# Scores of both heads in two adjacent PSUM banks, and one Exp over both, in a hybrid gMLP and attention decoder block

## The chip, the cores and the metric

The kernel runs on one Trainium2 chip, as one program on 8 cores. Each core has half of the sequence of one of the four batch entries (2048 positions) and takes the other half, or zeros, as the keys and values that lie before its own. The time is the device time in microseconds (us) of the slowest core.

## What is computed

One layer of a decoder block, cut to what matters here:

```python
h = _rmsnorm(x, norm_g[l])
proj = jnp.einsum('bsd,dn->bsn', h, w_in[l])
...
ya = _gmlp_sgu(a_u, a_v, a_ws[l], a_bs[l], a_ln_g[l], a_ln_b[l]) * jax.nn.silu(a_gate)
...
for p, (window, dilation) in enumerate(B_PATTERNS):      # (128, 1), (512, 4), (2048, 16)
    q = _rmsnorm(qkv[:, :, p, 0], qn_g[p])
    k = _rmsnorm(qkv[:, :, p, 1], kn_g[p])
    o, lse = _dilated_window(q, k, qkv[:, :, p, 2], window, dilation)
...
merged = jax.nn.sigmoid(g_a) * ya + jax.nn.sigmoid(g_b) * yb
x = x + jnp.einsum('bsd,de->bse', merged, w_out[l])
```

The attention is causal, over a window of 128 keys back at dilation 1, 4 or 16, with 8 heads of 64 columns; the outputs of the three patterns are mixed by their softmax denominators.

## The kernel before

The program is written out in order by Python, without a scheduler: each call of `c.op` (L95) puts one instruction on one engine and, where it depends on another engine, a wait on that engine's counter. PE, ACT and DVE run their own lists strictly in that order.

**Stages.** First the rows of x are normalised and transposed (`p0_task`, L343: ACT L354 to L358, DVE L360, eight PE transposes L370, DVE copy L372). Then come 12 attention steps, one for each of four pairs of heads (`hp`) and each of three patterns (`p`); they fill the profile to about 620 us. Behind them stand the gMLP branch (`a1_...`, `a2_task`), the merge (`c1_task`) and the output projection (`fin_task`).

**A step** (`step_tasks`, L432) is made of three kinds of task:

- a *q/k task* (`qk_task`, L386), 9 or 12 in a step: 8 matmuls of 512 columns into one bank (L300), ACT squares it (L393). Later its second part: one PE matmul L400 sums the squares into a second bank, ACT takes Ln (L402, from that bank) and Exp (L404), and DVE scales the first bank into `qT` or `kT` (L407). Only then are both banks given back.
- a *V task* (`v_s1`, L469), 5 or 8 in a step: 32 matmuls of 128 columns into one bank (L300), and DVE casts it into `Vaug` (L485).
- an *attention task* (`att`, L492), 8 in a step, 96 in all: 8 score matmuls L506 for a pair of blocks, those of head h into bank `sb[h]`; ACT takes Exp of each bank (L510, two activations of 128x512); DVE multiplies by the mask (L520, two). Later its second part: 8 matmuls L533 into one bank, which DVE copies or adds to `acc` (L543, L545).

**What sets the order.** `Pipe.submit` (L193) runs a task's first part and then the second parts that have become due; a q/k task's is due two tasks later, an attention task's three to five. The main loop (L687) lets the V and attention tasks of a step alternate with the q/k tasks of the next; every third task it slips in the end of a head pair (`fin_tasks`, ACT L587 to L589, DVE L590 to L594). Twelve of these ends lie inside attention steps.

**Banks.** PSUM has eight banks, in a `FreeList` (L175, L265): `get` takes the one that has been free longest, `put` adds one at the end.

```python
    def get(self):
        assert self.free, "pool exhausted (pipeline too deep for the buffer count)"
        return self.free.pop(0)
    def put(self, it):
        self.free.append(it)
```

`put` is called while the program is written, as soon as the bank's last reader has been recorded, so a bank can be handed out again long before that reader has run. The next PE group that writes it then waits on the chip for the reader (`_deps`, L86, takes in every reader of the buffer).

Of the kernel before, what the change touches and what calls it, by code (L numbers as in the profile page):

```python
# [5 lines left out]
F32 = mybir.dt.float32  # L6
BF16 = mybir.dt.bfloat16
ALU = mybir.AluOpType
AF = mybir.ActivationFunctionType


class Buf:
    __slots__ = ("name", "w", "r", "dsem", "dcnt")

    def __init__(self, name):
        self.name = name
        self.w = None
        self.r = []
        self.dsem = None
        self.dcnt = 0  # L20
# [154 lines left out]
class FreeList:  # L175
# [3 lines left out]
# [5 lines that stand above are left out]
        self.free.append(it)  # L184


class Pipe:

    def __init__(self):
# [43 lines left out]
def build_program(needed=None):  # L233
    nc = bass.Bass("TRN2", target_bir_lowering=False)
# [14 lines left out]
    c = Ctx(nc, needed)  # L249
    ar = Arena(nc)  # L250
    pipe = Pipe()
    PE, ACT, DVE, POOL, SP = c.pe, c.act, c.dve, c.pool, c.sp
    tn, sc, ve, gp = nc.tensor, nc.scalar, nc.vector, nc.gpsimd
# [8 lines left out]
            items.append((t_, b_))  # L262
        return FreeList(items), off

    banks = FreeList([(nc.alloc_psum_tensor(f"pb{i}", [128, 512], F32), Buf(f"pb{i}")) for i in range(8)])  # L265

    off = 0
    cb_t, b_cb, off = ar.alloc("cbf", [128, C_W], BF16, off)
# [163 lines left out]
    def step_tasks(hp, p, prefetch=True, buf=0, att_lag=3):  # L432
# [6 lines left out]
        if True:  # L439
# [51 lines left out]
            for q0 in range(0, len(qblocks), 2):  # L491
                def att(q0=q0):  # L492
                    pair = qblocks[q0:q0 + 2]
                    S = {}

                    def s1():
                        E, b_E0 = S["E"] = E_pool.get()
                        b_Eb = [b_E0, E_extra[id(b_E0)]]
                        sb = [banks.get(), banks.get()]
                        for bi, (r, cc) in enumerate(pair):  # L500
                            for pc in range(2):
                                for h in range(2):
                                    rows = slice(64 * h, 64 * h + 64)
                                    k0 = 128 * (cc + pc)
                                    o_ = (bi * 2 + pc) * 128
                                    c.op(PE, lambda: tn.matmul(sb[h][0][:, o_:o_ + 128], kv[rows, r, k0:k0 + 128],  # L506
                                                               qv[rows, r, 128 * cc:128 * cc + 128], start=True, stop=True),
                                         reads=[b_kT, b_qT], writes=[sb[h][1]], inc=(bi == len(pair) - 1 and pc == 1))
                        for h in range(2):
                            c.op(ACT, lambda: sc.activation(E[:, h].rearrange("p b c q -> p (b c q)"), sb[h][0][:],  # L510
                                                            AF.Exp, scale=8.0),
                                 reads=[sb[h][1]], writes=b_Eb)
                        for bi, (r, cc) in enumerate(pair):
                            mk = maskH if cc == 0 else maskN
                            ev = E[:, :, bi].rearrange("p h c q -> p h (c q)")
                            if False:
                                c.op(POOL, lambda: gp.tensor_tensor(ev, ev, mk.rearrange("p (h x) -> p h x", h=2), ALU.mult),
                                     reads=[b_Eb[bi], b_cb], writes=[b_Eb[bi]])
                            else:
                                c.op(DVE, lambda: ve.tensor_tensor(ev, ev, mk.rearrange("p (h x) -> p h x", h=2), ALU.mult),  # L520
                                     reads=[b_Eb[bi], b_cb], writes=[b_Eb[bi]])
                        banks.put(sb[0]); banks.put(sb[1])

                    def s2():
                        E, b_E0 = S["E"]
                        b_Eb = [b_E0, E_extra[id(b_E0)]]
                        po, b_po = banks.get()
                        for bi, (r, cc) in enumerate(pair):
                            for h in range(2):
                                for pc in range(2):  # L530
                                    blk = r * (nbo + 1) + cc + pc
                                    o_ = (bi * 2 + h) * 128
                                    c.op(PE, lambda: tn.matmul(po[:, o_:o_ + 128], Vaug[:, blk, h, :], E[:, h, bi, pc, :],  # L533
                                                               start=(pc == 0), stop=(pc == 1)),
                                         reads=[b_Vg[blk // 4], b_Eb[bi]], writes=[b_po],
                                         inc=(pc == 1 and h == 1 and bi == len(pair) - 1))
                        (r0, c0), (r1, c1) = pair
                        t00 = r0 + 128 * d * c0
                        t01 = r1 + 128 * d * c1
                        av = bass.AP(acc, t00, [pacc, [t01 - t00, 2], [T, 2], [d, 128]])  # L540
                        ov = po[:].rearrange("p (b h q) -> p b h q", b=2, h=2)
                        if p == 0:
                            c.op(DVE, lambda: ve.tensor_copy(av, ov), reads=[b_po], writes=[b_acc])  # L543
                        else:
                            c.op(DVE, lambda: ve.tensor_tensor(av, ov, av, ALU.add), reads=[b_po, b_acc], writes=[b_acc])  # L545
                        E_pool.put(S["E"]); banks.put((po, b_po))

                    need = max(r * (nbo + 1) + cc + 1 for (r, cc) in pair) // 4
                    return need, (lambda: pipe.submit(s1, s2, lag=att_lag, tag="att"))
                atasks.append(att())  # L550
            nv = 0
# [135 lines left out]
    for n in range(2, 12):  # L687
        hp, p = steps[n]
# [365 lines left out]
```

How the kernel before makes its waits and increments, by code:

```python
    def _wait(self, eng, toks):  # L64
        best = {}
        for t in toks:
            if t is None:
                continue
            sem, val, src = t
            if src is self.pe and eng is self.pe:
                continue
            k = id(sem)
            if eng.seen.get(k, 0) >= val:
                continue
            if k not in best or best[k][1] < val:
                best[k] = (sem, val, src)
        for k, (sem, val, src) in best.items():
            if src is None:
                actual = val
            else:
                self.waited.setdefault(src.name, set()).add(val)
                actual = val if self.rank is None else self.rank[src.name][val]
            eng.h.wait_ge(sem, actual)
            eng.seen[k] = val
# [10 lines left out]
    def op(self, eng, fn, reads=(), writes=(), inc=True):  # L95
        self._wait(eng, self._deps(reads, writes))
        ins = fn()
        if inc:
            eng.cnt += 1
            if self.needed is None or eng.cnt in self.needed.get(eng.name, ()):
                ins.then_inc(eng.sem, 1)
            tok = (eng.sem, eng.cnt, eng)
        else:
            tok = (eng.sem, eng.cnt + 1, eng)
        for b in reads:
            b.r.append(tok)
        for b in writes:
            b.w = tok
            b.r = []
        return tok
```

## Time and profile before

| | us |
|---|---|
| median of 3 runs (1087.00 to 1088.76) | 1087.82 |
| the profiled execution's own time | 1086.05 |
| its span on the slowest core, core 4 | 1085.0 |
| spans of the eight cores | 1074.1 to 1085.0 |
| PE busy | 959.8 |
| DVE busy | 607.5 |
| ACT busy | 536.6 |
| mean granted TensorE clock of the cores | 0.954 to 0.962 |

The span runs from the first to the last instruction of the program. A granted clock of 1 stands for 2.4 GHz, one of 0.5 for 1.2 GHz; between the two it is a mean over both. Busy time of PE is that of matmuls that overlap each other in the pipe, so eight matmuls of 512 columns stand as one row of 1.89 us at the full clock.

### The profile page before, as it was taken

The page shows a single profiled execution, that of the slowest core. Times are in us where ns is not written, and L with a number is a line of the kernel's source. Part 1 is how long each engine was busy: PE and PEld are TensorE (multiplying, and loading weights), DVE is VectorE, ACT ScalarE, POOL GpSimd, SP SyncE. Part 2 cuts the span into 40 slices and gives each one's busy share as a digit, 9 for nine tenths or more (in the row PEclk, how much of TensorE's full clock was granted, in tenths as well). Part 3 has the DMA queues.
Part 4 walks back from the last instruction along what each step waited for, and adds up shares of the span by engine and source line. Part 5 has one row for each costly group of instructions (what it writes and reads, how often), then busy time and mean ns, then how long its engine had stood idle before and what let it go on. Part 6 is the DMA issues. An engine that isn't in the chain of part 4 may idle for free.

```text
span 1085.0 us, 20753 instructions; the slowest of 8 cores (1074.1 to 1085.0 us)
## 1 busy us (share of the span) xinstructions
PE 959.8 (88%) x7264; PEld 543.4 (50%) x7264; DVE 607.5 (56%) x894; ACT 536.6 (49%) x946; POOL 161.9 (15%) x161
## 2 busy tenths in 40 slices
PE   2668769997899979999798978789999999999898
PEld 1336454664556646666466734444444344444343
DVE  6636794557675677756776766656553222222243
ACT  5656867657676686766866464443332111111100
POOL 2000000010000100000010000015454333331100
PEclk9779889999899998999999989889999999999999
DMA  9943521040330403303066000004453933441198
GB/s 237 212 100 60 117 69 18 4 41 1 31 31 2 40 2 30 31 2 30 1 89 79 1 1 1 1 1 40 40 54 52 94 34 35 46 47 11 59 293 270
DMA packets 101622, 62.57 MB, mean 58 GB/s; under 512 B 88720, under 2 KB 92816, under 8 KB 101520
## 3 DMA queue, kind: packets, MB, share of 16 engines
q0 software_dynamic: 91728, 26.61, 24.9%
q1 hardware_dynamic: 7344, 25.71, 7.1%
q10 hardware_dynamic: 2448, 8.91, 2.8%
q8 instruction: 61, 1.00, 0.4%
q14 instruction: 41, 0.34, 0.1%
HBM read 79.44 MB, written 8.39 MB: 81 GB/s over the span
## 4 chain that ended last, share of the span: by engine, by line
PE 67%; ACT 11%; DVE 9%; DMA 6%; issue 6%; DVEq 0%; POOL 0%; ACTq 0%; POOLq 0%; SPq 0%
PE pb L300 59%; DMA wr<-w_in 4%; PE pb L533 3%; ACT lr L402 3%; PE pb L506 2%; ACT lr L404 2%; DVE sta L745 2%; DVE hb L360 1%; PE pb L400 1%; DMA xt<-xh 1%; ACT junk L354 1%; PE pb L370 1%; ACT vg L743 1%; DMA wout<-w_out 1%; DVE kT L407 1%
## 5 line engine op out<-in xcount | busy, mean ns | idle before, releaser
L300 PE MATMUL pb<-hTo,wr 128*128 128x512 bf16 x1920 | 448.5, 386 | 14.6 <-DVE hTo L372 7.6
L300 PEld LDWEIGHTS pb<-hTo,wr 128*128 128x128 bf16 x1920 | 185.6, 99 | 231.0 <-issue 29.5
L119 POOL DMA_DIRECT2D wr<-w_in x72 | 63.8, 894 | 494.2 <-PE pb L300 226.3
L510 ACT ACTIVATE E<-pb 128x512 bf16<-128x512 f32 x192 | 113.0, 592 | 44.5 <-PE pb L506 34.5
L393 ACT ACTIVATE sq<-pb 128x512 bf16<-128x512 f32 (+1 forms) x120 | 69.7, 583 | 109.6 <-PE pb L300 108.1
L300 PE MATMUL pb<-wr,hTo 128*128 128x128 bf16 x1536 | 114.7, 230 | 2.1 <-DVE acc L543 1.9
L300 PEld LDWEIGHTS pb<-wr,hTo 128*128 128x128 bf16 x1536 | 104.0, 123 | 8.2 <-issue 5.1
L934 DVE SCALAR_TENSOR_TENSOR m<-ta,pb 128x512 f32<-128x512 f32 x32 | 22.0, 688 | 148.0 <-PE pb L300 148.0
L407 DVE SCALAR_TENSOR_TENSOR kT<-pb,cf,lr 128x512 bf16<-128x512 f32 (+1 forms) x72 | 70.6, 981 | 57.0 <-ACT lr L404 47.2
L520 DVE TENSOR_TENSOR E<-E,cbf 128x512 bf16<-128x512 bf16 x192 | 72.7, 420 | 30.2 <-ACT E L510 29.2
L402 ACT ACTIVATE lr<-pb,cf 128x512 f32<-128x512 f32 (+1 forms) x120 | 81.1, 676 | 5.4 <-PE pb L400 3.9
L404 ACT ACTIVATE lr<-lr 128x512 f32<-128x512 f32 (+1 forms) x120 | 74.6, 622 | 11.3 <-ACT lr L402 0.4
L927 ACT ACTIVATE ta<-pb 128x512 f32<-128x512 f32 x32 | 19.1, 597 | 120.6 <-PE pb L300 120.6
L407 DVE SCALAR_TENSOR_TENSOR qT<-pb,cf,lr 128x512 bf16<-128x512 f32 x48 | 47.4, 988 | 55.3 <-ACT lr L404 52.3
L545 DVE TENSOR_TENSOR acc<-pb,acc 128x512 f32<-128x512 f32 x64 | 72.3, 1130 | 1.4 <-PE pb L533 1.2
L837 POOL TENSOR_TENSOR gu<-gu,sa 128x512 f32<-128x512 f32 x32 | 40.7, 1271 | 186.5 <-ACT gu L824 130.4
L300 PE MATMUL pb<-wr,hTh 128*128 128x128 bf16 x672 | 57.9, 232 | 6.1 <-DVE acc L543 5.7
L533 PE MATMUL pb<-E,Vaug 128*128 128x128 bf16 x768 | 60.5, 224 | 2.5 <-DVE qT L407 1.6
L370 PE MATMUL pb<-cbf,hb 128*128 128x128 bf16 x256 | 25.6, 263 | 41.8 <-DVE hb L360 39.9
L506 PE MATMUL pb<-qT,kT 64*128 64x128 bf16 x768 | 42.4, 222 | 21.4 <-DVE kT L407 17.1
L300 PE MATMUL pb<-yaT,wr 128*128 128x512 bf16 x256 | 60.5, 379 | 0.0
L300 PE MATMUL pb<-Wv,hTo 128*128 128x512 bf16 x256 | 59.9, 392 | 0.0
(77 smaller groups left out, 1072.3 us busy)
## 6 DMA issues: line engine op xcount, KB each, us to landing
wr<-w_in POOLq DMA_DIRECT2D x72, 256.0 KB, 6.0
xt<-xh SPq DMA_DIRECT2D x16, 512.0 KB, 3.9
xf<-xo ACTq DMA_DIRECT2D x16, 512.0 KB, 5.4
out<-ot SPq DMA_DIRECT2D x16, 512.0 KB, 5.1
xt<-xo SPq DMA_DIRECT2D x12, 512.0 KB, 9.8
xtx<-xo SPq DMA_DIRECT2D x4, 512.0 KB, 12.3
Wv<-w_in POOLq DMA_DIRECT2D x2, 1024.0 KB, 10.9
wr<-w_oa POOLq DMA_DIRECT2D x8, 256.0 KB, 6.4
```

The costliest lines, as they stand in the source:

```text
L119: eng.h.dma_start(out=out, in_=in_, **kw).then_inc(owner.dsem, 16)
L300: c.op(PE, lambda kc=kc: tn.matmul(ps, lhs_fn(kc), rhs_fn(kc), start=(kc == 0), stop=(kc == nk - 1)), reads=reads, writes=[pbuf], inc=(kc ...
L393: c.op(ACT, lambda: sc.activation(sq[:, 0:n], ps[:, 0:n], AF.Square), reads=[b_ps], writes=[b_sq])
L402: c.op(ACT, lambda: sc.activation(lr[:, 0:n], ps2[:, 0:n], AF.Ln, bias=eps64_c, scale=1.0), reads=[b_ps2, b_cf], writes=[b_lr])
L404: c.op(ACT, lambda: sc.activation(lr[:, 0:n], lr[:, 0:n], AF.Exp, scale=-0.5), reads=[b_lr], writes=[b_lr])
L407: c.op(DVE, lambda: ve.scalar_tensor_tensor(dst, pv_, gcol, rv_, ALU.mult, ALU.mult), reads=[b_ps, b_lr, b_cf], writes=[dstB])
L506: c.op(PE, lambda: tn.matmul(sb[h][0][:, o_:o_ + 128], kv[rows, r, k0:k0 + 128], qv[rows, r, 128 * cc:128 * cc + 128], start=True, stop=True),
L510: c.op(ACT, lambda: sc.activation(E[:, h].rearrange("p b c q -> p (b c q)"), sb[h][0][:], AF.Exp, scale=8.0), reads=[sb[h][1]], writes=b_Eb)
L520: c.op(DVE, lambda: ve.tensor_tensor(ev, ev, mk.rearrange("p (h x) -> p h x", h=2), ALU.mult), reads=[b_Eb[bi], b_cb], writes=[b_Eb[bi]])
L533: c.op(PE, lambda: tn.matmul(po[:, o_:o_ + 128], Vaug[:, blk, h, :], E[:, h, bi, pc, :], start=(pc == 0), stop=(pc == 1)), reads=[b_Vg[blk ...
L545: c.op(DVE, lambda: ve.tensor_tensor(av, ov, av, ALU.add), reads=[b_po, b_acc], writes=[b_acc])
L837: c.op(POOL, lambda: gp.tensor_tensor(gu[:], gu[:], sa[:], ALU.mult), reads=[b_gu, b_sa], writes=[b_gu])
```

## The change

A class `PsumBanks` takes the place of the free list, in all of the kernel. PSUM is allocated as four tensors `pd0` to `pd3` of two banks each. `get_pair` looks for a tensor with both banks free. `get` looks first for a free bank whose neighbour is in use, and takes the one of these that has been free longest; only if there is none does it take the head of the list. An attention task asks for a pair, and where it gets one a single activation of 128x1024 takes Exp of both banks. Otherwise it works as before. The changed kernel's lines lie 28 lower (L300 is L328 there, L400 is L428, L506 is L535, L533 is L567), and L510 is L539.

```diff
--- before.py
+++ after.py
@@ -184,6 +184,34 @@
         self.free.append(it)
 
 
+class PsumBanks:
+
+    def __init__(self, nc):
+        self.dbl = [nc.alloc_psum_tensor(f"pd{k}", [128, 2, 512], F32) for k in range(4)]
+        self.items = {(k, i): (self.dbl[k][:, i, :], Buf(f"pb{k}{i}")) for k in range(4) for i in range(2)}
+        self.key = {id(it[1]): ki for ki, it in self.items.items()}
+        self.free = [(k, i) for i in range(2) for k in range(4)]
+
+    def get(self):
+        assert self.free, "PSUM banks exhausted (pipeline too deep)"
+        cands = [ki for ki in self.free if (ki[0], 1 - ki[1]) not in self.free]
+        ki = (cands or self.free)[0]
+        self.free.remove(ki)
+        return self.items[ki]
+
+    def get_pair(self):
+        for ki in self.free:
+            if (ki[0], 1 - ki[1]) in self.free:
+                k = ki[0]
+                self.free.remove((k, 0))
+                self.free.remove((k, 1))
+                return self.dbl[k], self.items[(k, 0)], self.items[(k, 1)]
+        return None
+
+    def put(self, item):
+        self.free.append(self.key[id(item[1])])
+
+
 class Pipe:
 
     def __init__(self):
@@ -262,7 +290,7 @@
             items.append((t_, b_))
         return FreeList(items), off
 
-    banks = FreeList([(nc.alloc_psum_tensor(f"pb{i}", [128, 512], F32), Buf(f"pb{i}")) for i in range(8)])
+    banks = PsumBanks(nc)
 
     off = 0
     cb_t, b_cb, off = ar.alloc("cbf", [128, C_W], BF16, off)
@@ -496,7 +524,8 @@
                     def s1():
                         E, b_E0 = S["E"] = E_pool.get()
                         b_Eb = [b_E0, E_extra[id(b_E0)]]
-                        sb = [banks.get(), banks.get()]
+                        pr = banks.get_pair()
+                        sb = [pr[1], pr[2]] if pr else [banks.get(), banks.get()]
                         for bi, (r, cc) in enumerate(pair):
                             for pc in range(2):
                                 for h in range(2):
@@ -506,10 +535,15 @@
                                     c.op(PE, lambda: tn.matmul(sb[h][0][:, o_:o_ + 128], kv[rows, r, k0:k0 + 128],
                                                                qv[rows, r, 128 * cc:128 * cc + 128], start=True, stop=True),
                                          reads=[b_kT, b_qT], writes=[sb[h][1]], inc=(bi == len(pair) - 1 and pc == 1))
-                        for h in range(2):
-                            c.op(ACT, lambda: sc.activation(E[:, h].rearrange("p b c q -> p (b c q)"), sb[h][0][:],
+                        if pr:
+                            c.op(ACT, lambda: sc.activation(E[:].rearrange("p h b c q -> p h (b c q)"), pr[0][:],
                                                             AF.Exp, scale=8.0),
-                                 reads=[sb[h][1]], writes=b_Eb)
+                                 reads=[sb[0][1], sb[1][1]], writes=b_Eb)
+                        else:
+                            for h in range(2):
+                                c.op(ACT, lambda: sc.activation(E[:, h].rearrange("p b c q -> p (b c q)"), sb[h][0][:],
+                                                                AF.Exp, scale=8.0),
+                                     reads=[sb[h][1]], writes=b_Eb)
                         for bi, (r, cc) in enumerate(pair):
                             mk = maskH if cc == 0 else maskN
                             ev = E[:, :, bi].rearrange("p h c q -> p h (c q)")
```

No instruction changes its place on an engine. What moves is the bank that each PE group writes, and with it the wait in front of the group. Below, `pb` and `pd` are the banks and the two-bank tensors, `sq` the squares, `wr` the weights of a projection, `hTo` and `hTh` the transposed rows, E the attention weights, and `[waits ...]` names the engines' counters (`s_act`, `s_dve`, `s_pe`) or a DMA's (`d_...`) in front of a row.

PE, in the step of pattern 1 of the second head pair, the stretch from which the round of the timeline below comes (q/k tasks of the next step between its V and attention tasks), before:

```order
L400 MATMUL pb6<-sq0_16_59,cbf_1_43 128x512 [waits s_act]
L300 MATMUL pb7<-wr7_12_54,hTo_4_46 128x128 [waits s_dve]
L300 MATMUL pb7<-wr7_12_54,hTo_4_46 128x128 x31
L300 MATMUL pb1<-hTo_4_46,wr1_6_48 128x512 [waits s_dve]
L300 MATMUL pb1<-hTo_4_46,wr1_6_48 128x512 x7
L533 MATMUL pb4<-E0_44_89,Vaug_23_66 128x128 [waits s_act]
L533 MATMUL pb4<-E0_44_89,Vaug_23_66 128x128 x7
```

The same place with the change, with the q/k group two rows ahead of it:

```order
L328 MATMUL pd3<-hTo_4_46,wr1_6_48 128x512 [waits s_dve]
L328 MATMUL pd3<-hTo_4_46,wr1_6_48 128x512 x7
L428 MATMUL pd2<-sq0_16_59,cbf_1_43 128x512 [waits s_act]
L328 MATMUL pd3<-wr7_12_54,hTo_4_46 128x128 [waits s_dve]
L328 MATMUL pd3<-wr7_12_54,hTo_4_46 128x128 x31
L328 MATMUL pd3<-hTo_4_46,wr1_6_48 128x512 [waits s_dve]
L328 MATMUL pd3<-hTo_4_46,wr1_6_48 128x512 x7
L567 MATMUL pd2<-E0_44_89,Vaug_23_66 128x128 x8
```

Before, each group writes a bank that was last used five or more groups earlier. With the change the L428 matmul, the V group and the next q/k group take banks that were given back just ahead: the V group writes the bank that L407 of the preceding L428 reads last, and the q/k group the bank that the V cast reads.

PE at the next attention task of the same stretch, before:

```order
L400 MATMUL pb5<-sq1_17_60,cbf_1_43 128x512 [waits s_act]
L506 MATMUL pb3<-qT_14_57,kT_15_58 128x128
L506 MATMUL pb2<-qT_14_57,kT_15_58 128x128 [waits s_dve]
L506 MATMUL pb3<-qT_14_57,kT_15_58 128x128
L506 MATMUL pb2<-qT_14_57,kT_15_58 128x128
L506 MATMUL pb3<-qT_14_57,kT_15_58 128x128
L506 MATMUL pb2<-qT_14_57,kT_15_58 128x128
L506 MATMUL pb3<-qT_14_57,kT_15_58 128x128
L506 MATMUL pb2<-qT_14_57,kT_15_58 128x128
L300 MATMUL pb6<-hTo_4_46,wr1_6_48 128x512 [waits s_act]
L300 MATMUL pb6<-hTo_4_46,wr1_6_48 128x512 x7
```

And with the change:

```order
L428 MATMUL pd0<-sq1_17_60,cbf_1_43 128x512 [waits s_act]
L535 MATMUL pd0<-qT_14_57,kT_15_58 128x128 [waits s_act]
L535 MATMUL pd0<-qT_14_57,kT_15_58 128x128 x7
L328 MATMUL pd3<-hTo_4_46,wr1_6_48 128x512 [waits s_dve]
L328 MATMUL pd3<-hTo_4_46,wr1_6_48 128x512 x7
```

The score matmuls now write the tensor that L428 has just written and wait for its reader L402; the q/k group behind them waits for L407 of the same L428.

ACT at the first attention task of a step, before (its two Exps are rows of their own):

```order
L393 ACTIVATE sq2_18_61<-pb0 128x512 [waits s_pe]
L510 ACTIVATE E0_44_89<-pb1 128x512 [waits s_pe]
L510 ACTIVATE E0_44_89<-pb6 128x512 [waits s_pe,s_act]
```

And with the change:

```order
L421 ACTIVATE sq2_18_61<-pd0 128x512 [waits s_pe]
L539 ACTIVATE E0_44_89<-pd1 128x1024 [waits s_pe]
```

All 96 attention tasks get a pair: the changed program has 96 activations of 128x1024 in the place of 192 of 128x512.

## Rows read from the trace of the kernel before

**Rows 1.** The page: busy time of the engines, share of the span, instructions.
```profile
PE 959.8 (88%) x7264; PEld 543.4 (50%) x7264; DVE 607.5 (56%) x894; ACT 536.6 (49%) x946; POOL 161.9 (15%) x161
```

**Rows 2.** Windows, the attention steps and what follows: busy us, (instructions), granted clock, DMA.
```profile
60.00:620.00 560.00, 502.17 (x5051) 330.21 (x5052) 378.23 (x561) 378.63 (x665) 35.07 (x40) 0.95 0.27 36
620.00:1085.00 465.00, 433.94 (x2060) 198.45 (x2058) 191.47 (x300) 125.71 (x207) 118.95 (x108) 0.97 0.37 63
```

**Rows 3.** Waits of PE from 60 to 620 us: total us, times, longest.
```profile
PE pb L506 <- DVE kT L407: 17.1, 13, 3.0
...
PE pb L300 <- ACT E L510: 4.6, 6, 0.8
PE pb L506 <- ACT E L510: 2.5, 6, 0.5
```

**Rows 4.** Groups by form: count, busy us, mean ns, idle before.
```profile
L510 ACT ACTIVATE E<-pb 128x512 bf16<-128x512 f32 x192 | 113.0, 592 | 44.5 <-PE pb L506 34.5 <-ACT E L510 1.1 <-DVE E L520 0.3
L402 ACT ACTIVATE lr<-pb,cf 128x512 f32<-128x512 f32 x116 | 79.7, 687 | 5.4 <-PE pb L400 3.9
...
L520 DVE TENSOR_TENSOR E<-E,cbf 128x512 bf16<-128x512 bf16 x192 | 72.7, 420 | 30.2 <-ACT E L510 29.2 <-issue 0.2
...
L402 ACT ACTIVATE lr<-pb,cf 128x128 f32<-128x128 f32 x4 | 1.5, 371 | 0.0
```

**Rows 5.** Timeline, one q/k task's second part: start us, us, engine, instruction.
```profile
179.73 0.38 PE L400 MATMUL pb<-sq,cbf 128*128 128x512 bf16 x1
...
180.49 0.68 ACT L402 ACTIVATE lr<-pb,cf 128x512 f32<-128x512 f32 x1
181.26 0.63 ACT L404 ACTIVATE lr<-lr 128x512 f32<-128x512 f32 x1
...
182.06 1.08 DVE L407 SCALAR_TENSOR_TENSOR kT<-pb,cf,lr 128x512 bf16<-128x512 f32 x1 [0.87 <-PE pb L400]
```

**Rows 6.** Timeline, one round of V, q/k, attention and q/k tasks.
```profile
300.63 1.08 DVE L407 SCALAR_TENSOR_TENSOR kT<-pb,cf,lr 128x512 bf16<-128x512 f32 x1 [0.68 <-ACT lr L404]
...
301.40 0.38 PE L400 MATMUL pb<-sq,cbf 128*128 128x512 bf16 x1
...
301.85 1.50 PE L300 MATMUL pb<-wr,hTo 128*128 128x128 bf16 x24
...
303.19 0.61 PE L300 MATMUL pb<-wr,hTh 128*128 128x128 bf16 x8
...
303.64 1.89 PE L300 MATMUL pb<-hTh,wr 128*128 128x512 bf16 x8
...
304.66 0.68 DVE L485 CAST Vaug<-pb 128x512 bf16<-128x512 f32 x1
...
305.36 0.38 PE L400 MATMUL pb<-sq,cbf 128*128 128x512 bf16 x1
...
306.00 1.90 PE L300 MATMUL pb<-hTo,wr 128*128 128x512 bf16 x8
...
307.43 1.27 ACT L510 ACTIVATE E<-pb 128x512 bf16<-128x512 f32 x2
```

**Rows 7.** Timeline, a head pair's end inside a step, on ACT and DVE.
```profile
259.77 0.63 ACT L589 ACTIVATE ty<-ty 128x512 f32<-128x512 f32 x1
...
260.51 0.68 DVE L590 TENSOR_TENSOR ty<-ty,acc 64x512 f32<-64x512 f32 x1 [0.95 <-ACT ty L589]
```

**Rows 8.** Windows, columns as in rows 2: PE with pauses, and what follows.
```profile
30.90:71.90 41.00, 22.56 (x137) 13.24 (x136) 22.41 (x25) 23.29 (x53) 0.88 (x1) 0.67 0.94 180
265.00:273.30 8.30, 5.94 (x72) 3.85 (x69) 5.19 (x9) 6.05 (x12) 0.28 (x1) 1.00 0.00 0
273.30:280.10 6.80, 4.68 (x46) 4.47 (x47) 6.21 (x12) 5.35 (x10) 2.35 (x3) 0.50 0.99 91
```

**Rows 9.** Timeline of PE: a wait ahead of rows 8's third row; eight matmuls at 1.2 GHz.
```profile
271.54 0.38 PE L506 MATMUL pb<-qT,kT 64*128 64x128 bf16 x7 [1.74 <-DVE kT L407]
62.80 3.57 PE L300 MATMUL pb<-hTo,wr 128*128 128x512 bf16 x8 [7.60 <-DVE hTo L372]
```

## The prediction

> **What bounds it now.** I read the page first: PE is busy 88% of the span, DVE 56%, ACT 49% [rows 1]. Then windows: in the attention steps, 60 to 620 us, PE works 502 of 560 us at a mean clock of 0.95, DVE 378 and ACT 379 us [rows 2]. So PE bounds the stretch that the change touches, and ACT, on which it saves, has a third of its time free there. Then PE's waits: what it waits for longest is the last `kT` of a step, 17.1 us; for Exps (L510) it waits 4.6 and 2.5 us in all [rows 3]. A cheaper Exp has about 7 us of PE's time to win. The timeline of one round shows why the waits are short: PE hands over a bank and goes on, and ACT and DVE follow several groups behind. The V group starts at 301.85 although the L407 that runs up to 301.71 belongs to an L400 five groups back in the program's order [rows 6].
>
> **The change: one Exp for two.** One activation of 512 columns takes 592 ns [rows 4]. Ln shows what columns cost: 687 ns for 512, 371 ns for 128 [rows 4], 0.82 ns each, so 1024 columns take about 0.59 + 0.42 = 1.01 us. The two stand as 1.27 us now [rows 6]. The saving is 0.26 us on ACT for each of 96, 25 us; bounds are 0 (two banks cost what two instructions do) and 0.34. As ACT does not bound, I take 5 us of it for PE, out of the 7. Against it, the first bank of the pair is free only at the end of the long Exp, 0.4 us later; the banks of the scores are reused late in both kernels, so that costs nothing.
>
> **The change: who gets which bank.** This is the larger part. Before, a bank comes back after all others that were free; followed through the whole program, no PE group writes a bank whose last reader hangs on one of the three groups before it; four groups back is the nearest, six the most common. The new `get` prefers the bank whose neighbour is in use. While one bank of a tensor is held, its other half is handed out, given back, and handed out again at once, as the two places in the order above show. Counted over the program, 220 handouts then hang on the group just before (or two before), nearly all ahead of 620 us. There PE must wait until ACT and DVE have finished with work that it has only just given them. By kind:
>
> - *A group behind L400 that takes a bank of the same q/k task.* The reader is L407. From the end of L400 (180.11) through L402 and L404 to the end of L407 (183.14) are 3.03 us [rows 5]; PE starts 0.14 us after a reader's end (301.71 to 301.85) [rows 6]: 3.17 us. Before, PE went on after 0.07 us (301.78 to 301.85), so 3.10 us are added. There are 48: 149 us.
> - *The same with the scores or an output group between,* which in 24 cases themselves wait for L402. Before, the next q/k group starts 0.26 us after L400's end (305.74 to 306.00) [rows 6]; now 3.17: 2.91 us, 42 times: 122 us.
> - *A group behind a V group, in the same bank or its neighbour's place,* waits for the cast: 0.17 (L404 to L407 [rows 5], as the hand-over), 0.68 [rows 6] and 0.14 us, where before it overlapped the V group's end by 0.16: 1.15 us, 47 times: 54 us.
> - *L400 behind an output group L533, for its copy to `acc`,* 10 times, mostly where a head pair's end is queued. From the end of the L400 before, ACT is through L404 after 1.8 us [rows 5]; three more at 0.72 (0.63 and a gap of 0.09) and the Exp of 1.0 follow; DVE begins L590 behind L589 at 4.0 us, does three at 0.79 (0.68 and 0.11) [rows 7], two masks at 0.42 [rows 4] and the copy, priced as the cast at 0.68 [rows 6]: done at 8.0, PE on at 8.1 us. L533 had started at 3.17 and run 0.6: the wait is 4.3, with the lost overlap 4.5 us: 45 us.
> - *Other groups behind an output group:* 22 at about 2 us (two masks, a copy or add of at least 0.68, both hand-overs): 44 us. The rest, 18 waits for transposes' copies and L402 and 9 single ones, at 0.7 us: about 20 us.
>
> Together 434 us. Of the waits of before 24 us (17.1 + 4.6 + 2.5) are no longer separate [rows 3]: 410, rounded down for waits that nest. I take **400 us of added waits** at the full clock, between 330 (waits that nest more than I count) and 460.
>
> The Trainium skill, "Perfetto Trace Analysis", section Optimizing Tensor Performance, says that independent matmul groups should rotate through different PSUM banks so that the evacuation of one overlaps the next group. By it the sum keeps the 400 us; by the words of the change alone, Exp is cheaper and nothing else moves, it would be -5.
>
> **The change: the clock.** PE's pauses cost more than themselves. From 265 to 273.3 us it is granted in full, and PE is busy 5.94 of 8.30 us, with a wait of 1.74 us in it; from there to 280.1 us the clock is 0.50, that is 1.2 GHz [rows 8, 9]. At 1.2 GHz eight matmuls take 3.57 us [rows 9] against 1.89 at 2.4 GHz [rows 6]. The nearest row to a PE that pauses in every round is 30.9 to 71.9 us: busy 22.56 of 41 us, mean clock 0.67 [rows 8]. With 400 us of waits PE would be busy about half of the steps, in pieces of 2 to 5 us. I take that row's clock. Of the 560 us some 22 are what the low clock costs already (a tenth of the time, PE busy four fifths of it, half of that). At 0.67, two thirds of the stage's time T are at 1.2 GHz; with PE busy 0.6 of them that is 0.4 T of slow matmuls, half of it added: T = 560 - 22 + 400 + 0.2 T, so T = 1172, which is 612 more than now. Bounds: at the clock of before T = 960; with all of PE's 480 us at 1.2 GHz T = 938 + 480 = 1418.
>
> The Trainium skill, "TensorE: Matmul & The Clock Gate", section A second HAM failure mode, tells of a kernel whose cycling through its PSUM queue let PE idle so often that its clock swung between the levels. The rows at 273 us agree in kind; what its rate is in these steps no row shows.
>
> **Sum.** 1086 (the profiled execution's own time) + 612 gives 1698; less the few us of Exp and with the median 2 us above that execution: **1700 us**. The change itself ends where it began in the stages behind 620 us: there banks come back long before their turn (9 handouts of the 220), and I add nothing.
>
> **Rivals.**
>
> 1. *The waits come, the clock holds.* For it: the pauses are 3 us at most, and pieces of full work lie between them. Against it: rows 8. Time 1086 + 400 = 1486, with a tenth of slow time as now 1490.
> 2. *Half of the waits are hidden,* because PE's groups still queued elsewhere let it fall less far behind ACT and DVE than I count: 1086 + 200 = 1286. Against it: PE takes its groups strictly in order, so nothing can fill a wait.
> 3. *Faster.* The place is the bank's hand-over. If the readers of a bank just returned were already done when PE arrives, no wait forms, and only the Exp is left: 1086 - 5 to -7, 1080. It decides in this way where ACT and DVE finish within PE's own hand-over of 0.07 us; rows 5 show 3.03 us, so it would need the allocator to work otherwise than it reads.
> 4. *The change doesn't do what it says:* no pair is free and the old two Exps run. In the program's order all 96 get one. It would move 5 us, not the waits.
>
> **Chances.** Forecast 0.66 (1560 to 1850, by the clock), clock holds 0.20, half hidden 0.09, faster 0.03, other 0.02. The range is 1470 to 1850: it takes in the second case and leaves out the last three, and the top of the forecast's bounds. A measurement of this kernel can tell about 0.2% from no change. Faster 0.03, same 0.01, slower 0.96.
>
> **What would show it.** In the profile after: the Exp group 96 times at about 1.0 us. PE's waits for `kT` and `qT` (L407) grow from some 20 us to over 200 us and lead its list; waits for the `Vaug` cast, not in its list now, come with some 50 us, those for `acc` with some 80. The 60 to 620 us stretch becomes over 1000 us long, with PE busy at about 60% and a clock near 0.7; what follows keeps its 465 us. ACT's and DVE's busy times hardly change. If the waits are there and the clock stays above 0.9, rival 1 has it. If PE's waits stay below 100 us, the count by program order is wrong as a measure of waits.

## The result and the profile after

The changed kernel takes 1604.81 us (median of 8 runs, 1602.15 to 1606.82) against 1087.14 us: a ratio of 1.4761 (1.4745 to 1.4777). It is 48% slower. The prediction said 1700 us, from 1470 to 1850. In some executions of these kernels the cores of a die run at a lower clock and take some per cent longer; such executions are left out of all times and ratios here.

The page of the changed kernel, its slowest core, against [rows 1] and the page's clock digits (2 is busy tenths in 40 slices):

```profile
span 1603.8 us, 20103 instructions; the slowest of 8 cores (1586.2 to 1603.8 us)
PE 1120.0 (70%) x7154; PEld 621.9 (39%) x7264; DVE 612.0 (38%) x894; ACT 530.9 (33%) x850; POOL 161.9 (10%) x161
PE   2466666666656566656566756568697999899999
PEclk9678876877677758877777876878898999999999
```

ACT has its 96 instructions less, and its busy time fell from 536.6 to 530.9 us; DVE works as before (612.0 against 607.5 us). PE stands for a third of the first 28 slices and its clock is low in most of them. 110 of this core's matmuls have no record (7154 of 7264), so what follows is read from core 2, whose span is 1598.2 us and whose records are all there.

Windows of core 2, the same two pieces of the program as in [rows 2] (columns as there):

```profile
60.00:1125.00 1065.00, 680.41 (x5045) 412.99 (x5046) 382.01 (x560) 373.16 (x571) 35.02 (x40) 0.76 0.14 19
1125.00:1598.00 473.00, 437.12 (x2075) 198.88 (x2072) 193.24 (x302) 126.43 (x208) 118.71 (x108) 0.97 0.36 62
```

The attention steps grew from 560 to 1065 us. Of these 505 us, PE stands for 327 more (1065 - 680 = 385, before 560 - 502 = 58), and it is busy for 178 more with the same matmuls, at a clock of 0.76 in place of 0.95. What follows took 465 and takes 473 us.

What PE waited for on core 2 (total us, times, longest), against [rows 3]:

```profile
PE pd L328 <- DVE qT L435: 94.5, 34, 4.6
PE pd L328 <- DVE kT L435: 84.3, 38, 3.2
PE pd L428 <- DVE acc L577: 34.7, 10, 3.9
...
PE pd L328 <- DVE Vaug L513: 26.4, 28, 0.9
PE pd L535 <- ACT lr L430: 25.4, 24, 1.2
PE pd L428 <- DVE kT L435: 14.3, 5, 3.2
PE pd L535 <- DVE Vaug L513: 12.5, 9, 2.3
PE pd L567 <- DVE qT L435: 11.7, 4, 3.1
PE pd L535 <- DVE acc L579: 10.9, 4, 3.2
PE pd L567 <- DVE kT L435: 9.4, 6, 1.6
...
PE pd L328 <- DVE acc L579: 8.2, 4, 2.7
PE pd L567 <- DVE Vaug L513: 7.5, 8, 0.9
...
PE pd L535 <- DVE acc L577: 6.3, 3, 2.2
PE pd L328 <- DVE acc L577: 6.1, 7, 1.0
...
PE pd L428 <- DVE acc L579: 3.8, 3, 1.3
```

Of the pairs that wait 20 times or more, none stood in the list of before but for one wait of 0.2 us for `kT`. L435 is the L407 of before: the rows on it make 214 us. The 72 waits of its first two rows are also what the count by program order gives for L328 behind L435: 42 handouts that hang on the group just before and 30 that hang on the one before that. The 24 waits for L430 are the 24 for L402, the 28 are the 28 q/k groups in the V group's own bank, the 10 are the 10 copies to `acc`.

One such wait in the timeline of core 2 (start us, us), to be read against [rows 5] and [rows 6]:

```profile
702.07 0.38 PE L428 MATMUL pd<-sq,cbf 128*128 128x512 bf16 x1
...
702.82 0.68 ACT L430 ACTIVATE lr<-pd,cf 128x512 f32<-128x512 f32 x1
703.60 0.63 ACT L432 ACTIVATE lr<-lr 128x512 f32<-128x512 f32 x1
704.40 1.11 DVE L435 SCALAR_TENSOR_TENSOR kT<-pd,cf,lr 128x512 bf16<-128x512 f32 x1 [2.48 <-ACT lr L432]
...
705.65 1.95 PE L328 MATMUL pd<-wr,hTo 128*128 128x128 bf16 x32 [3.20 <-DVE kT L435]
707.70 0.69 DVE L513 CAST Vaug<-pd 128x512 bf16<-128x512 f32 x1 [2.20 <-PE pd L328]
708.54 1.89 PE L328 MATMUL pd<-hTo,wr 128*128 128x512 bf16 x8 [0.94 <-DVE Vaug L513]
```

PE stands 3.20 us from the end of L428, until the last reader of the bank that the V group takes over has run; then it stands 0.94 us for the cast of that V group. DVE itself was idle for 2.48 us ahead of the first and 2.20 us ahead of the second: neither engine bounds, they take turns.

The Exp of before [rows 4] is now this group (count, busy us, mean ns, idle before), on the slowest core. Its busy time was 113.0 us:

```profile
L539 ACT ACTIVATE E<-pd 128x1024 bf16<-128x1024 f32 x96 | 97.7, 1018 | 72.0 <-PE pd L535 56.5 <-DVE Vaug L513 15.1
```

### The profile page after: what moved, and what is told of

Its sections match the earlier page's. It is cut to its first block, busy times and chain, and to the rows that moved or that the text cites. A ratio compares the mean times of both kernels' runs of the same rounds, so it can differ in the third digit from the quotient of the medians.

```text
span 1603.8 us, 20103 instructions; the slowest of 8 cores (1586.2 to 1603.8 us)
## 1 busy us (share of the span) xinstructions
PE 1120.0 (70%) x7154; PEld 621.9 (39%) x7264; DVE 612.0 (38%) x894; ACT 530.9 (33%) x850; POOL 161.9 (10%) x161
## 4 chain that ended last, share of the span: by engine, by line
PE 61%; ACT 14%; DVE 13%; issue 8%; DMA 3%; DVEq 0%; ACTq 0%; POOL 0%; another core or an unknown queue 0%; POOLq 0%
PE pd L328 55%; ACT lr L430 4%; ACT lr L432 3%; DVE kT L435 3%; DMA wr<-w_in 3%; PE pd L567 2%; DVE Vaug L513 2%; DVE qT L435 2%; PE pd L535 1%; ACT sq L421 1%; DVE acc L579 1%; PE pd L428 1%; DVE E L554 1%; ACT junk L382 1%; DVE acc L577 1%
## 5 line engine op out<-in xcount | busy, mean ns | idle before, releaser
L328 PE MATMUL pd<-hTo,wr 128*128 128x512 bf16 x1860 | 513.3, 433 | 119.3 <-DVE kT L435 31.9
L328 PEld LDWEIGHTS pd<-hTo,wr 128*128 128x128 bf16 x1920 | 199.6, 107 | 368.3 <-issue 204.7
L421 ACT ACTIVATE sq<-pd 128x512 bf16<-128x512 f32 (+1 forms) x120 | 70.4, 586 | 509.5 <-PE pd L328 509.5
L328 PE MATMUL pd<-wr,hTo 128*128 128x128 bf16 x1536 | 149.9, 271 | 71.1 <-DVE qT L435 43.4
L328 PEld LDWEIGHTS pd<-wr,hTo 128*128 128x128 bf16 x1536 | 134.6, 139 | 81.6 <-issue 81.5
L435 DVE SCALAR_TENSOR_TENSOR kT<-pd,cf,lr 128x512 bf16<-128x512 f32 (+1 forms) x72 | 70.0, 972 | 165.8 <-ACT lr L432 165.8
L539 ACT ACTIVATE E<-pd 128x1024 bf16<-128x1024 f32 x96 | 97.7, 1018 | 72.0 <-PE pd L535 56.5
L430 ACT ACTIVATE lr<-pd,cf 128x512 f32<-128x512 f32 (+1 forms) x120 | 81.0, 675 | 94.3 <-PE pd L428 43.5
L435 DVE SCALAR_TENSOR_TENSOR qT<-pd,cf,lr 128x512 bf16<-128x512 f32 x48 | 46.9, 976 | 156.9 <-ACT lr L432 151.1
L328 PE MATMUL pd<-wr,hTh 128*128 128x128 bf16 x672 | 71.8, 268 | 42.0 <-DVE kT L435 26.2
L535 PE MATMUL pd<-qT,kT 64*128 64x128 bf16 x768 | 44.8, 244 | 71.6 <-ACT lr L430 26.5
L567 PE MATMUL pd<-E,Vaug 128*128 128x128 bf16 x768 | 72.9, 251 | 29.7 <-DVE qT L435 11.6
L567 PEld LDWEIGHTS pd<-E,Vaug 128*128 128x128 bf16 x768 | 61.3, 115 | 54.4 <-issue 48.5
L328 PE MATMUL pd<-hTh,wr 128*128 128x512 bf16 (+1 forms) x185 | 56.3, 464 | 34.3 <-DVE qT L435 14.0
L328 PEld LDWEIGHTS pd<-wr,hTh 128*128 128x128 bf16 x672 | 60.5, 150 | 42.6 <-issue 41.1
L428 PE MATMUL pd<-sq,cbf 128*128 128x512 bf16 (+1 forms) x96 | 44.0, 461 | 43.8 <-DVE acc L577 23.6
```

The source lines that it names most:

```text
L328: c.op(PE, lambda kc=kc: tn.matmul(ps, lhs_fn(kc), rhs_fn(kc), start=(kc == 0), stop=(kc == nk - 1)), reads=reads, writes=[pbuf], inc=(kc ...
L421: c.op(ACT, lambda: sc.activation(sq[:, 0:n], ps[:, 0:n], AF.Square), reads=[b_ps], writes=[b_sq])
L430: c.op(ACT, lambda: sc.activation(lr[:, 0:n], ps2[:, 0:n], AF.Ln, bias=eps64_c, scale=1.0), reads=[b_ps2, b_cf], writes=[b_lr])
L435: c.op(DVE, lambda: ve.scalar_tensor_tensor(dst, pv_, gcol, rv_, ALU.mult, ALU.mult), reads=[b_ps, b_lr, b_cf], writes=[dstB])
L539: c.op(ACT, lambda: sc.activation(E[:].rearrange("p h b c q -> p h (b c q)"), pr[0][:], AF.Exp, scale=8.0), reads=[sb[0][1], sb[1][1]], wr ...
```

## The experiments

Two theories stood against each other. By the first, the order in which banks are handed out costs the time: PE waits for readers it has only just supplied, and its clock falls with the pauses. The rivals were that reading two banks with one instruction costs, that reusing banks costs in PSUM itself, and that the low clock is hidden inside the waits and adds nothing. The kernel before ran beside each group of versions: 1085.6 us beside the a versions, 1101.3 us beside the b versions and 1086.9 us beside the c versions, and ratios are to it. The b versions ran on another chip: in b1 and b2 the stages behind the attention, which no version touches, show a clock of 0.92, against 0.97 in [rows 2]. b1, b3, b4 and c1 stand on a single execution each, without an interval.

**The banks as they are, two Exps (a1).**

```diff
-                        if pr:
-                            c.op(ACT, lambda: sc.activation(E[:].rearrange("p h b c q -> p h (b c q)"), pr[0][:],
-                                                            AF.Exp, scale=8.0),
-                                 reads=[sb[0][1], sb[1][1]], writes=b_Eb)
-                        else:
+                        if True:
                             for h in range(2):
```

> The changed kernel with its banks handed out as they are, but each bank of a pair read by an Exp of its own (192 of 128x512). Theory (the order of the banks costs the time): 1600 to 1615 us, PE's waits for L407's instruction about 190 us as in the changed kernel; the two Exps give back at most 15 us of ACT's saving where ACT stands in the chain of waits. Rival (an activation that reads two banks at once holds PE or DVE up): back to 1090 to 1200 us.

Measured: 1609.2 us (1608.3 to 1614.9), ratio 1.4837 (1.4807 to 1.4867). Its waits of PE on its slowest core, all records there:

```profile
PE pd L328 <- DVE qT L435: 94.4, 34, 4.6
PE pd L328 <- DVE kT L435: 84.3, 38, 3.2
PE pd L428 <- DVE acc L573: 34.5, 10, 3.8
```

They are the waits of the changed kernel to 0.2 us. The rival on the wide Exp falls: without it nothing comes back. The single Exp even saves 8 us here (1.4761 against 1.4837 of 1087), more than the 5 us below. That ACT stands in the chains here would explain it, but no run separates this.

**The bank that has been free longest, the pair that has been free longest (a2, and a3 with two Exps).** 96 of 96 pairs are still granted.

```diff
-        cands = [ki for ki in self.free if (ki[0], 1 - ki[1]) not in self.free]
-        ki = (cands or self.free)[0]
+        ki = self.free[0]
...
-        for ki in self.free:
-            if (ki[0], 1 - ki[1]) in self.free:
-                k = ki[0]
...
+        ks = [k for k in range(4) if (k, 0) in self.free and (k, 1) in self.free]
+        if not ks:
+            return None
+        k = min(ks, key=lambda k: max(self.free.index((k, 0)), self.free.index((k, 1))))
```

> The single Exp over a pair kept, get() takes the bank that has been free longest and get_pair the full tensor that has been free longest: all 96 pairs are still granted, and 3 handouts instead of 220 hang on one of the two groups before. Theory: 1078 to 1092 us, no wait of PE for the V cast, its waits for L407's instruction back to some 20 us. Rival (the pair itself costs): over 1150 us.

> The same banks as in the oldest-first version, with two Exps of 128x512. Theory: 0 to 8 us slower than with one Exp (25 us less work on ACT, which does not bound, and 7 us of PE's waits for Exps), 1083 to 1095 us. Rival (ACT bounds the steps after all): 20 us or more slower than with one Exp.

Measured: with one Exp 1080.5 us, 0.9952 of before (0.9939 to 0.9966); with two 0.9996 (0.9984 to 1.0007). Waits of PE in the steps (60 to 612 us) on core 1 of the version with one Exp:

```profile
PE pd L538 <- DVE kT L438: 13.8, 7, 3.0
PE pd L538 <- ACT E L542: 9.4, 9, 1.5
PE pd L401 <- DVE hb L391: 9.2, 10, 2.1
PE pd L331 <- DVE acc L580: 8.4, 9, 2.3
```

The cast and L402 are gone from the list, and the waits for L407 (L438 here) are back at 16 us with the smaller rows, 20 before. So the choice in `get` and `get_pair` carries the 48%, and the idea of the change, one Exp for two, is worth 0.44%, about 5 us, once they are right. This version is faster than both kernels, and than the one before by 0.3 to 0.6%. The 5 us did not come the way the prediction put it, from PE's waits for Exps: those are 9.4 us here against 7.1 [rows 3]. The longest wait in the steps of before, for `kT`, is 3.3 us smaller, but it is 13.9 us in a3 too: that comes with the banks and not with the Exp. From the first Exp of the steps to the last one, a2 takes 522.1 us, a3 527.8 and the kernel before 528.2 (medians of the eight cores). So the gain lies in the steps and needs the single Exp; how it gets to PE is left open.

**Rest for returned banks (b1, b2, b3).** `get` passes over a bank until one (b1) or two (b2) other handouts have followed its return; b3 does it, with two, only for the banks of q/k tasks.

```diff
-        cands = [ki for ki in self.free if (ki[0], 1 - ki[1]) not in self.free]
+        rested = [ki for ki in self.free if self.n - self.back.get(ki, -99) >= 1]
+        cands = [ki for ki in rested if (ki[0], 1 - ki[1]) not in self.free]
...
```

> The changed kernel, but get() passes over a bank until one other handout has followed its return. 134 handouts instead of 220 hang on one of the two groups before (L407 69, cast 13, output copies 13). Counted as in the prediction, with the PE work that now lies between taken off, added waits fall from 385 us to 195 us. Theory: the time per counted us of wait stays as measured (519 us for 385, so 1.35): 1350 us, between 1290 and 1410. Rival (only the number of such handouts counts): 1088 + 519 x 134/220 = 1404 or more; rival (it is L407's chain alone): 1088 + 519 x 145/240 = 1401.

> The same, but two other handouts must have followed. 49 such handouts, counted waits 95 us. Theory: 1088 + 1.35 x 95 = 1216 us if the clock falls with them as in the changed kernel, 1183 us if the pauses are now too few for that; 1160 to 1240.

> Only the banks that a q/k task gives back are passed over until two other handouts have followed. L407's handouts fall from 90 to 14, the cast's from 47 to 14 along with them (the order shifts), output copies 26. Counted waits 144 us, of which L407 45. Theory: 1088 + 1.35 x 144 = 1282 us (1220 to 1330). Rival (the casts and copies, not L407, carry the time): above 1400.

Measured. "Handouts" are those that hang on one of the two groups before. "Counted waits" are the sum of the prediction with the PE work that lies between taken off (385 us for the changed kernel, where the prediction had 434).

| version | handouts | counted waits us | time us | ratio | clocks of the cores |
|---|---|---|---|---|---|
| changed kernel | 220 | 385 | 1604.8 | 1.476 | 0.820 to 0.834 |
| b1 | 134 | 195 | 1313.3 | 1.192 | 0.891 to 0.898 |
| b3 | 83 | 144 | 1283.8 | 1.166 | 0.877 to 0.907 |
| b2 | 49 | 95 | 1198.0 | 1.088 (1.0854 to 1.0904) | 0.914 to 0.939 |
| a2 | 3 | about 6 (3 at 2 us) | 1080.5 | 0.995 | 0.953 to 0.960 |

The time goes down in the order of the counted waits, and in the order of the handouts as well: either count of the program's order ranks the versions without a run. They part only at b1. In proportion to its handouts it would take 1404 us, by L407's part alone 1401, by its counted waits 1350, and it took 1313. For b3 (1284 against 1282) and b2 (1204 against 1216) the two counts give nearly the same, so that waits count and not handouts rests on b1. b3's rival, above 1400 us, falls. The price per counted us isn't one figure: 518/385 = 1.35 for the changed kernel, and by their own ratios (times 1088) 209/195 = 1.07 for b1, 180/144 = 1.25 for b3, 96/95 = 1.01 for b2. The expectation of 1.35 was too dear for all three. b2 came out at the second of its two expected times, 1183 us, for pauses too few to pull the clock down (1088 + 96 is 1184), and the 0.91 of its steps is hardly under the 0.92 behind them. b3 has what b1 has fewer of, copies to `acc` behind a head pair's end; its longest wait of PE is of that kind, 6.0 us on average where the prediction put 4.5, so its count is too low:

```profile
PE pd L433 <- DVE acc L582: 54.3, 9, 6.1
```

**The chain alone, in the kernel before (c2).** Its banks and its Exps are untouched; PE is only made to wait for L407 behind each of the 120 q/k second parts.

```diff
     def op(self, eng, fn, reads=(), writes=(), inc=True):
-        self._wait(eng, self._deps(reads, writes))
+        toks = self._deps(reads, writes)
+        if eng is self.pe and self.force is not None:
+            toks.append(self.force)
+            self.force = None
+        self._wait(eng, toks)
...
                  reads=[b_ps, b_lr, b_cf], writes=[dstB])
+            c.force = dstB.w
```

> The kernel before, with its own banks in its own order and its two Exps; only a wait is added: the first PE instruction behind each of the 120 q/k second parts waits for that part's L407. The disputed chain by itself. Theory (the time comes from PE waiting for the work it has only just handed over): 120 x about 2.9 us = 350 us of waits less 20 us that they replace, and 1.35 us of time for each: 1088 + 1.35 x 330 = 1533 us, 1460 to 1600; mean clock below 0.88. Rival (the reuse of banks costs in another way, such as in how PSUM is accessed): at most 1088 + 330 = 1420 us, with a clock of 0.93 or more.

Measured: ratio 1.4233 (1.4208 to 1.4259), 1546 us, clocks 0.841 to 0.853. The window of the steps on its slowest core, to be read against [rows 2], and its two largest waits of PE (L413 is L407 here; all rows on it make 359 us):

```profile
60.00:1078.00 1018.00, 643.52 (x5052) 397.48 (x5053) 382.35 (x562) 392.69 (x667) 35.03 (x40) 0.78 0.14 20
```

```profile
PE pb L513 <- DVE kT L413: 105.3, 35, 4.3
PE pb L306 <- DVE qT L413: 101.6, 29, 9.5
```

PE stands for 1018 - 644 = 374 us where it stood for 58, and is busy 141 us longer at 0.78. No bank is reused sooner than before, and yet 460 us are lost, of the changed kernel's 518: with 120 chains of L407 where that has 90, and without its waits for casts and copies. So the waiting alone costs this much, with nothing changed in PSUM. The rival's bound of 1420 us is passed by far, and its clock of 0.93 missed.

**Matmuls in the waits (b4 and c4 with 8, c3 with 4; c1 is the changed kernel beside them).** The banks are those of the changed kernel. Behind 90 of the L428 (a list in the program, `FILL`, names them), matmuls of constants go into the bank that has been free longest, and nothing reads them.

```diff
+            if nqk[0] in FILL:
+                fk, (ft, b_f) = banks.free[0], banks.items[banks.free[0]]
+                for _ in range(8):
+                    c.op(PE, lambda: tn.matmul(ft, bdones, cb_t[:, 0:512], start=True, stop=True),
+                         reads=[b_cb], writes=[b_f])
+            nqk[0] += 1
```

> The changed kernel with the same banks, and behind each of the 90 L400 matmuls (L428 there) whose q/k banks are handed out at once, 8 matmuls of 512 columns of constants into the bank that has been free longest; nothing reads them. At 2.4 GHz they take 1.7 us of the 3.1 us that PE stands there anyway. They are added work, the results are the same. Theory (the low clock adds PE time of its own, 160 us by the two profiles): the mean clock rises from 0.82 to 0.88 or more, the time falls to 1450 to 1560 us. Rival (the chains of waits set the time and the low clock is hidden in them): 1600 us or more, since 90 x 1.7 us of work come on top where they don't fit.

> The changed kernel once more, for comparison on the chip of the three others of this call. 1600 to 1630 us, mean clock 0.82.

> As the version with 8 idle-time matmuls, with 4 of them (0.86 us at 2.4 GHz in each of the 90 waits of 3.1 us). Theory (the clock falls with how long PE stands): between the two, 1520 to 1600 us, mean clock 0.84 to 0.90. Rival (any matmul in the wait keeps the clock up): as with 8, below 1515 us.

> The version with 8 idle-time matmuls again, beside the changed kernel on one chip: 90 to 120 us faster than it, clock 0.92, as in its first profile (1497 us against 1604 us).

Measured: the changed kernel 1603.5 us; with 4 matmuls a ratio of 1.4036 (1.4006 to 1.4067), 1523 to 1527 us; with 8 one of 1.3651 (1.3622 to 1.3681), 1483 us, and 1496.9 us in b4 on the slower chip. The steps in their windows, with 8 and then with 4:

```profile
60.00:1005.00 945.00, 707.72 (x5779) 413.90 (x5780) 384.98 (x562) 376.62 (x572) 35.06 (x40) 0.92 0.16 22
```

```profile
60.00:1050.00 990.00, 681.12 (x5432) 405.38 (x5431) 384.55 (x564) 375.25 (x572) 35.04 (x40) 0.86 0.15 21
```

720 matmuls more, and 120 us less. The added ones are busy for 173 us of the 708, which leaves 535 us for the kernel's own work where it had 680; with 4 it is 97 of 681 us, which leaves 584. One wait with its filling, in the version with 8 (timeline of PE; L442 are the added ones):

```profile
501.68 0.63 PE L430 MATMUL pd<-sq,cbf 128*128 128x512 bf16 x1
502.10 2.50 PE L442 MATMUL pd<-cbf 128*128 128x512 bf16 x8
504.88 0.68 PE L328 MATMUL pd<-wr,hTh 128*128 128x128 bf16 x8 [0.27 <-DVE qT L437]
```

PE works through 2.5 us of the wait and stands for 0.27 us; the V group still starts when the reader is done. The chains are there as before: standing and filling together make 410 us (237 + 173), where PE stood for 385. So the chains give nothing back, and what is gained is the clock: 0.76 in the steps of the changed kernel, 0.86 with 4, 0.92 with 8. The rival that hides the low clock in the waits falls, and so does the one for c3: 4 matmuls keep the clock up only in part.

## Why the prediction was right

*The mechanism.* The change's worth was put into the order of the banks and not into the Exp, and that held: a2 takes the order away and keeps the Exp, a1 does the reverse, c2 has the chain alone. The Exp came out at 1018 ns, forecast 1.01 us. ACT's and DVE's busy times and the stages behind (473 us for 465) hardly moved, as forecast. One size in it was off without weight for the result: 25 us were to be saved on ACT, and the group's busy time fell by 15 us (113.0 to 97.7), ACT's in all by 6. The pair's row of 1.27 us had a pause between its two Exps in it, so a pair does end 0.25 us sooner. Of the signs, PE busy at about 60% came out at 64%, and the clock near 0.7 at 0.76.

*The waits, by kind.* Forecast for L407 and L402, 149 + 122 = 271 us; measured 214 + 25 = 240. For the casts 54; measured 46 (26.4 + 12.5 + 7.5). For the copies and adds to `acc` 45 + 44 = 89; measured 70. All rows together make 385 us, where the kinds made 434. In all PE stands for 327 us more, where the sum said 400. One part of the gap is that the sum took off 24 us for waits of before, where PE had stood for 58 in all. The larger part is the added time per wait: with the scores between (42 cases) 2.91 us were put down as if PE did nothing meanwhile, though it works through 0.4 us of scores or 0.6 us of an output group; the waits behind a head pair's end are 3.5 us on average, not 4.5; and those behind other output groups 1.7 us (35 us in 21), not 2.

*The clock.* Forecast 0.67 from the nearest row, and 212 us for it; measured 0.76 and 178 us. That the term came out so near is luck, because two factors in it were wrong in opposite directions. The share of time at 1.2 GHz was put at two thirds; by a mean of 0.76 it is 0.48, or 511 us. PE was taken to be busy for 0.6 of that. But its busy time grew from 480 us of work at the full clock (502 less the 22) to 680, so 200 us were added by matmuls at half speed, and those took 400 us: 0.78 of 511. The clock records in core 2's trace say the same directly: 519 us of the steps are at 1.2 GHz, and PE is busy in 404 of them. The product is 0.38 T where 0.4 T was forecast. With the measured values the prediction's own equation is T = 560 - 22 + 327 + 0.19 T = 1068, against 1065 measured; with the measured waits and the forecast's 0.2 T it is 1081. So of the 107 us by which T was too long, some 90 come from the waits. The row of 30.9 to 71.9 us was a poor neighbour: there PE stands for 45% of the time, in the steps for 36%.

*The rivals.* "The clock holds" gave 1490 us against 1605, with waits that were 73 us too large; the windows show 178 us more of PE's time at the lower clock, and filling the waits gives 120 us back. "Half of the waits are hidden" came true for none of the kinds. "Faster" would have needed the readers to be done in 0.07 us; they took 3.20. The Trainium skill's rule on rotating groups through the banks (Perfetto Trace Analysis, Optimizing Tensor Performance) is borne out with a size here: from 0.995 to 1.476 of the time, by the order of the handouts alone. The Trainium skill's account of a clock that swings with such cycling (TensorE: Matmul & The Clock Gate, A second HAM failure mode) fits the steps' 0.76: core 2's trace has 83 stretches at 1.2 GHz in them, with full clock between.

## What to carry to other kernels

An allocator that favours the buffer returned last, for locality, packing or adjacency, takes the engine that runs ahead back to the pace of its followers; take the one that has been free longest, and look for adjacency only among those. Before a run, count for each handout how many groups back the one lies that the last reader hangs on: here four and more were harmless (the kernel before), and one or two cost from 0.9 us (a cast) to 3.2 us (L407's chain) each, and more behind a head pair's end. Where PE must stand, add what its clock loses: here 0.54 us for each us that it stood longer in the changed kernel (178 for 327), and 0.45 in c2 (141 for 316).

## What the runs showed of the hardware

- Work put into a wait can pay: 720 matmuls that nobody reads took 120 us off a kernel of 1603 us, because PE's granted clock in the steps rose from 0.76 to 0.92; half as many took 80 us off, at 0.86.
- The price of a wait was not one figure: 1.01 us of time for each counted us at 95 us (b2), 1.07 at 195 (b1), 1.25 at 144 (b3), 1.39 at 330 (c2, 459 us) and 1.35 at 385. The granted clock was 0.914 and more in b2 and 0.82 in the changed kernel.
- One activation over two adjacent banks takes 1018 ns against two of 592: 0.17 us less busy time, and in a2 against a3 no other cost was seen.
